# Attention with V stationary and spread reciprocals, and with the merge's operand splits placed while attention and merge run

## What is computed

```python
h = rms_norm(x, norm1_g) * (1 + sc1) + sh1
qa, ka, va, qb, kb, vb, ga, gb = jnp.split(h @ w_in, SPLIT_POINTS, axis=-1)
# global attention: 8 query heads on 2 key/value heads of 64, softmax over all keys of the group
oa = global_attention(rope(qa), rope(ka), va) @ w_branch_a
# windowed attention: a tile of queries sees its own and the two neighbour tiles, with a bias and a sink
ob = window_attention(qb * 64**-0.5, kb, vb, rel_bias, sink) @ w_branch_b
merged = jax.nn.sigmoid(ga) * oa + jax.nn.sigmoid(gb) * ob
x = x + gt1 * (merged @ w_out)
h2 = rms_norm(x, norm2_g) * (1 + sc2) + sh2
x = x + gt2 * expert_choice_moe(h2, ...)      # 16 experts, 160 rows each
y = rms_norm(x, norm_f_g)
```

## Time and profile before

| | us |
|---|---|
| median of 3 runs | 2703.78 |
| lowest and highest run | 2701.26, 2705.55 |
| the profiled execution, its own time | 2707.09 |
| its span | 2705.0 |
| TensorE busy | 2472.5 (91%) |
| DVE, ACT, POOL busy | 1634.4, 1168.9, 1016.8 |

### The profile page before, as it was taken

The page is one execution under the profiler, slowest core; times in us unless marked ns, Lnnn a source line. Parts: engine busy times, 40 slices in busy tenths (PEclk is TensorE's granted clock), DMA queues, the critical chain, the costliest instruction groups (busy, mean ns, idle before and its releaser), DMA issues.

```text
span 2705.0 us, 53532 instructions
## 1 busy us (share of the span) xinstructions
PE 2472.5 (91%) x23338; PEld 1817.1 (67%) x23428; DVE 1634.4 (60%) x2045; ACT 1168.9 (43%) x1461; POOL 1016.8 (38%) x641
## 2 busy tenths in 40 slices
PE   6999899999879999994389999999999999999994
PEld 2444578876645555553388888888888888888872
DVE  2443355544541111557588887888888888888872
ACT  2111244444531110233155556555656555566552
POOL 0000000000003232103365766676766677766640
PEclk8999699997989999996699999999999999999997
DMA  8000200012030110335288999999999999999965
GB/s 306 16 24 1 86 1 1 1 63 94 32 102 24 47 47 0 117 117 186 82 288 315 322 334 321 320 319 333 320 332 319 319 326 330 328 325 321 313 258 183
DMA packets 230112, 512.20 MB, mean 189 GB/s; under 512 B 7820, under 2 KB 35581, under 8 KB 229757
## 3 DMA queue, kind: packets, MB, share of 16 engines
q1 hardware_dynamic: 219324, 477.36, 49.8%
q0 software_dynamic: 10560, 31.46, 4.2%
HBM read 480.49 MB, written 28.31 MB: 188 GB/s over the span
## 4 chain that ended last, share of the span: by engine, by line
PE 86%; DVE 7%; ACT 2%; DMA 2%; issue 2%; SPq 1%; POOL 1%; DVEq 0%; ACTq 0%; POOLq 0%
PE ps L1337 20%; PE ps L1338 19%; PE ps L1336 19%; PE ps L1405 8%; PE ps L1472 6%; PE ps L1607 3%; PE ps L1459 3%; PE ps L1440 3%; PE ps L1450 1%; DVE arena L981 1%; DVE ti_s L990 1%; DVE top_s L989 1%; DVE arena L991 1%; PE ps L1370 1%; PE ps L1544 1%
## 5 line engine op out<-in xcount | busy, mean ns | idle before, releaser
L1337 PE MATMUL ps<-arena 128*128 128x160 bf16 (+2 forms) x5344 | 1311.2, 264 | 23.4 <-issue 8.0
L1338 PE MATMUL ps<-arena 128*128 128x160 bf16 (+2 forms) x5343 | 1310.4, 264 | 0.0
L1336 PE MATMUL ps<-arena 128*128 128x160 bf16 (+2 forms) x5255 | 1277.7, 262 | 14.9 <-DVE arena L1270 7.2
L1237 DVE TENSOR_TENSOR arena<-arena 128x2048 bf16<-128x2048 f32 x376 | 922.0, 2457 | 189.1 <-ACT arena L737 188.4
L737 ACT ACTIVATE arena<-arena 128x2048 bf16<-128x2048 f32 x384 | 726.4, 1904 | 237.1 <-PE ps L1338 180.6
L1336 PEld LDWEIGHTS ps<-arena 128*128 128x128 bf16 x5344 | 524.8, 98 | 164.4 <-issue 38.0
L1338 PEld LDWEIGHTS ps<-arena 128*128 128x128 bf16 x5344 | 524.9, 98 | 129.1 <-issue 4.2
L1337 PEld LDWEIGHTS ps<-arena 128*128 128x128 bf16 x5344 | 524.9, 98 | 120.3 <-issue 3.6
L620 POOL TENSOR_TENSOR arena<-arena 128x512 f32<-128x512 f32 (+1 forms) x24 | 26.1, 1086 | 989.9 <-DVE arena L1177 989.9
L661 POOL TENSOR_TENSOR arena<-arena 128x320 bf16<-128x320 f32 x128 | 277.8, 2170 | 10.0
L658 POOL TENSOR_TENSOR arena<-arena,ones 128x320 bf16<-128x320 f32 x128 | 182.4, 1425 | 184.2 <-DVE arena L1270 184.0
(11 more groups left out here) (192 smaller groups left out, 2211.9 us busy)
## 6 DMA issues: line engine op xcount, KB each, us to landing
arena<-w_e_gate SPq DMA_DIRECT2D x64, 2048.0 KB, 8.9
arena<-w_e_up SPq DMA_DIRECT2D x64, 2048.0 KB, 9.4
arena<-w_e_down SPq DMA_DIRECT2D x64, 2048.0 KB, 8.9
arena<-w_ada SPq DMA_DIRECT2D x12, 2048.0 KB, 8.2
arena<-x_sample SPq DMA_DIRECT2D x16, 512.0 KB, 3.5
arena<-w_in SPq DMA_DIRECT2D x16, 512.0 KB, 4.6
arena<-w_in SPq DMA_DIRECT2D x3, 2048.0 KB, 16.8
arena<-w_out SPq DMA_DIRECT2D x2, 2048.0 KB, 9.2
```

The lines of the kernel that those rows point to most:

```text
L1237: ve.tensor_tensor(lo, stage_half(kind, a), hi, ALU.subtract).then_inc(lo_done, 1)
L1336: pe.matmul(out, w_hi, x_hi, start=start, stop=False)
L1337: pe.matmul(out, w_hi, x_lo, start=False, stop=False)
L1338: return pe.matmul(out, w_lo, x_hi, start=False, stop=stop)
```

## The change

- `PV`: `V` (128x64) becomes stationary and `PT` (128 columns) moving. The two heads go to the two column halves of the array, alternating within each key tile. Bank 4 now has the head's channels on the partitions, which is the layout that `OT` made before.
- The reciprocals then have to lie along the free dimension. New step `RB`: DVE takes the reciprocal as soon as the group's exponentials are done, and POOL spreads it to 128x512 (one tensor_tensor). `OT` becomes four float32 matmuls with that tile stationary and the identity moving; ACT copies their result to `on`. `NM` on DVE multiplies bank 4 with it. `OT` now stands ahead of the last `PV` of its group.
- The bfloat16 split of the attention output goes from ACT and DVE to POOL (two tensor_tensor for each group), and so does the split of `h`: ten pairs of 128x1024, at every odd item from 51 to 69.
- `AR` stands at every second item from 34 to 48, and `AC` right behind the next item's `S` and `MX`.
- The first merge weights are loaded before attention and split behind item 80's copies, ahead of the last item's. `GT` moves behind output tile 0. `WO` 1 is done with `WO` 0, before the last chunk of the merge, and output tile 0 waits for the first 23 chunks only.
- `PT` of B and other buffers get places of their own.

```diff
@@ plan_steps
-    for i in range(len(items) + 5):
+    for i in range(len(items) + 4):
...
+        copies = [("TE",) + x[1:] for x in parts]
+        done = i - (4 if i <= first_b + 4 else 5)
+        if done >= 0 and done % NPAIR == 0 and done < len(items) and (done < first_b) == (i <= first_b + 4):
+            s.append(("RB", done // NPAIR))
...
         if i < len(items):
             s += [("S", i), ("MX", i)]
+        if s_ac < c:
+            s.append(("AC", s_ac))
+            s_ac += 1
...
-        if ready:
+        if pv < len(items) and pv <= (t - 2 if parts else t - 1):
+            if pv % NPAIR == NPAIR - 1:
+                s.append(("OT", pv // NPAIR))
             s.append(("PV", pv))
             pv += 1
...
-        if i >= first_b + 2 and i % 4 == 2 and c < 12:
+        if i >= first_b - 6 and i % 2 == 0 and c < 12:
             s.append(("AR", c))
             c += 1
-    s.append(("A2",))
...
+        if i >= first_b + 11 and i % 2 and hs < NT:
+            s.append(("HS", hs))
+            hs += 1
+        if i == len(items):
+            s += [("A2",), ("WS", 0)]
...
+                if k == "RB":
+                    g = s[1]
+                    if g:
+                        gp.wait_ge(t_done, job_at[(("OT", g - 1), 0)] + 1)
...
+                    gp.wait_ge(rinv_ready, g + 1)
+                    gp.tensor_tensor(rb_of(g).rearrange("p (h d) -> p h d", d=HD),
+                                     ones[:, 0:HD].unsqueeze(1).to_broadcast([P, 8, HD]),
+                                     rinv[:, g % 2].unsqueeze(2).to_broadcast([P, 8, HD]), ALU.mult).then_inc(rb_ready, 1)
...
+                if k == "HS":
...
+                    gp.tensor_tensor(hTs[:, 0:KD, a:z], hT[:, :, a:z], ones[:, 0:KD].unsqueeze(2).to_broadcast([P, KD, P]),
+                                     ALU.mult).then_inc(hs_hi, 1)
+                    gp.wait_ge(hs_hi, t + 1)
+                    gp.tensor_tensor(hTs[:, KD:2 * KD, a:z], hT[:, :, a:z], hTs[:, 0:KD, a:z], ALU.subtract).then_inc(hs_done, 1)
...
                 if k == "NM":
                     g = s[1]
...
+                    ve.wait_ge(rb_copied, g + 1)
                     ve.wait_ge(pv_done, NPAIR * (g + 1))
...
+                    ve.tensor_tensor(on_of(g), ps[:, 4], on_of(g), ALU.mult).then_inc(o_norm, 1)
...
-                            ins = pe.matmul(ps[:, 4, o:o + HD], PT[:, i % 2, hh, n, :], V[:, br, kt, hh * HD:hh * HD + HD],
-                                            start=(n == 0), stop=(n == len(kts) - 1))
+                    for n, kt in enumerate(kts):
+                        for hh in range(2):
+                            ins = pe.matmul(ps[hh * 64:hh * 64 + 64, 4, j * P:(j + 1) * P],
+                                            V[:, br, kt, hh * 64:hh * 64 + 64], PTs[br][:, i % 2, hh, n, :],
+                                            start=(n == 0), stop=(n == len(kts) - 1), tile_position=(0, 64 * hh))
...
-                    pe.wait_ge(o_norm, g + 1)
+                    pe.wait_ge(rb_ready, g + 1)
...
-                        ins = pe.transpose(b[:, j * P:(j + 1) * P], oh[:, g % 2, j * P:(j + 1) * P], ident[:])
+                        ins = pe.matmul(b[:, j * P:(j + 1) * P], rb_of(g)[:, j * P:(j + 1) * P], ident[:],
+                                        start=(j == 0), stop=True, skip_group_check=True)
```

## The result

The changed kernel takes **2605.7 us** (median of 4 runs, 2604.1 to 2607.1) beside 2702.5 us (2699.8 to 2705.6) for the kernel before on the same chip: a ratio of 0.9641, 95% interval 0.9625 to 0.9658. The forecast was 2620 us with a range of 2597 to 2665: sign and range held, and it was 14 us too careful.

What follows compares the result with a forecast made beforehand. TensorE's work was taken to bound A, and a chain of TensorE, ACT and DVE to bound B. From 2703.8 us, -35.4 (A) - 31.3 (B) - 17.7 (to the merge) + 0.6 = -83.8 gave 2620, range 2597 to 2665.

Steps and rivals of the forecast that it cites:

- B: Later stretch of attention, where TensorE, ACT and DVE wait for each other: forecast -31.3 us in all.
- 16 rounds and a switch: `PV` in A: column halves run side by side, 16 x 0.11 plus tile-shape switch, about 2.04 us, 1.47 less.
- A: Sample part of attention with TensorE full: forecast -35.4 us, including about -3.5 for the first items.
- The first nine items: Start of attention, called first ten items in the prediction: `PV` of 8 records at half clock, about -3.5 us.
- I take a third of the half-clock loss back, -6: Clock term in B: TensorE moves as many columns in less time, -6 us, bounds +15 and -15.
- the five `AC`: Term in B: the other five `AC` no longer stand ahead of scores, freeing about 1 us each, -5.
- It fits, barely: POOL in B: 12.4 us of work for four items against the 13.3 us they should take.
- The rival: POOL becomes B's bound: passes 2.9 times as long beside DVE, +108 us, about 2728; chance 0.05.
- To the merge: From attention's last scores to the merge's first chunk: about 14.5 us instead of 32.2, -17.7.
- From the merge to the output: `GT` behind output tile 0 costs 3.5 us; tile 0 not waiting for the last chunk saves 3; +0.6.
- the halves didn't take turns: Rival on `PV`: its column halves take turns, so it keeps 3.5 us and pays the switch, +67, 2687; chance 0.08.
- the first rival: TensorE's clock falls in B: half the last 32 items at half clock +30, 2650; all, 2686; chance 0.15.

Runs made afterwards that it cites:

- e1: The changed kernel with each item's `PV` matmuls issued all for the even head first, then all for the odd head, not alternating: 2653.1 us.
- p2: The kernel before with only the `V`-stationary `PV` and alternating column halves, its output scaled and laid out wrongly: 2639.4 us.
- p1: The kernel before with only `AR` moved to every second item from 34 to 48 and `AC` right behind the scores: 2698.6 us.
- e2: The changed kernel with `AC` issued at the end of the iteration again, behind the values: 2604.9 us.
- e6: The changed kernel with the split of `h` taken from POOL and put back on ACT and DVE behind attention, in three pieces: 2614.6 us.
- e5: The changed kernel with POOL doing each split of `h` twice: 2636.3 us.
- e9: The changed kernel with the first merge weights loaded after the last values and split at the end of attention's steps: 2615.4 us.
- e8: The changed kernel with `OT` right behind the scores and the last `RB` ahead of the first merge weights' split: 2592.3 us.
- e7: The changed kernel with `OT` issued right behind the scores and maxima, its ACT copy ahead of the exponentials: 2597.7 us.

## Why the prediction was right, and where it was off

**`PV`.** Right, and for the reason given. 16 rounds and a switch were to take 2.04. `PV` fills 1.90 and the transposes on either side take 0.14 longer than in the earlier trace rows (0.58 and 1.46 from start to start, in place of 0.49 and 1.41), so together they are the 2.04. The item is 5.86 (forecast 5.87), and e1 shows it is the alternation of halves that does it. The choice between the two rows, `AR` in column groups against the old `PV`, was the decision of this case. The rule of the Trainium skill that stood against it (TensorE: Matmul & The Clock Gate, Part 3, "The mechanism"), taken as strictly as the prediction put it, is not what these runs show: both orders of e1 and after use all rows, and alternating column halves alone brought 3.25 down to 1.90.

**A.** Right: -32.2 against -31.9. An item with `OT` takes 6.80 (forecast 6.9), `AR` and `AC` together 2.9 in A, as in the earlier trace rows.

**The first nine items.** Term mis-sized: -8.9 against -3.5. The stretch of half clock in which attention starts is 20.5 us shorter. Before, and after:

```profile
292.60:333.60 41.00, 32.14 (x128) 23.73 (x130) 15.83 (x47) 13.38 (x44) 0.00 (x0) 0.50 0.34 121
```

```profile
293.60:314.10 20.50, 12.22 (x54) 7.60 (x54) 9.72 (x33) 7.60 (x23) 0.00 (x0) 0.50 0.96 301
```

The prediction took half clock for all these items as given. p2 and e1 both have the short stretch, p1 doesn't: V stationary brings it, in either order. Beside that, `PV` itself is some 0.7 us shorter at half clock in both (1.05 and 1.06 in place of 1.74). How the -8.9 divide between the two wasn't measured, and why the clock rises sooner stays open.

**B.** Direction right, one step too small: -41.4 against -31.3. The rhythm was met (13.37 us for four items at the end of B, forecast 13.3; two items 6.19, forecast 6.1 to 6.6), `AR` and `AC` alone gave 13.0 (p1; forecast 9.3 and 5), the values alone 14.1 (p2; forecast 8 and 3). The failing step is "I take a third of the half-clock loss back, -6": all of it came back, B has no half clock left where it had 54.6 us, and what neither part brings alone is 14.3. Which piece of the change does that stays open. The reason given for the five `AC` isn't the right one: standing ahead of the scores costs nothing in the changed kernel (e2), where they stand in other items than `OT` but for one; the wait that they shed was for a bank behind `OT` (p1, p2).

**POOL.** "It fits, barely" holds (11.4 us of work, forecast 12.4, in the 12.3 us of the fastest four items), and e6 shows a cover without any leak. The rival had its place right, as e5 shows from doubled splits on; its price rested on a row of POOL beside a DVE pass with two `arena` operands, which B hardly has: in B the passes took 1.04 and 1.16 for 512 columns, as alone, and 1.90 and 2.13 for 1024.

**To the merge.** Right: 15.25 against 14.5, -16.9 against -17.7. e6 and e9 confirm the two covers. The wait that was named, the last reciprocal behind DVE's pass over the weights, was called free since the chunk "needs the weights anyway". It wasn't: DVE's pass ended at 672.4, the first chunk came at 676.8, and e8 gained 4.5 us by taking this wait away.

**From the merge to the output.** -2.1 against +0.6. TensorE's 4.58 us wait for POOL ahead of the output is gone; in its place stand two of 1.27 and 1.10 for DVE's split of `w_out`. `GT` costs 4.0 at full clock, 0.5 more than forecast. These don't add up to -2.1, and the rest wasn't looked into.

**The rivals.** The clock didn't fall in B, the halves didn't take turns (e1 shows what that would have cost: 47 us and not 67), POOL didn't bind. The worst end of the first rival was added up wrongly: 32 items at 1.9 us more give 2681, not 2686; and `OT` in A comes to +2.8 by its own numbers, not +3.0. The wait that was named last, `NM` behind ACT's copy, is there with 1.86 us, but late in B it doesn't hold up the next maximum as feared; what `OT`'s place cost was 8 us (e7), at least in part on TensorE.

## What to carry to other kernels

Matmuls whose weights lie in different column halves ran nearly side by side here when they alternated (1.90 us in place of 3.25), so two narrow outputs are worth interleaving step by step, and not one after the other. A prediction of a stretch with pauses should be made once at full and once at half clock, since removing pauses can bring back the whole difference and not a share of it. Work moved to an idle engine was free here at 93% of the loop's period and cost all that stood over beyond it, so compare its sum with the period; and where a long pass moves ahead of a short one that starts a chain over three engines, put the short one first. A wait in the trace isn't a cost by itself: look whether the instruction behind it would have waited for something else anyway, as with `NM` here.

## What the runs showed of the hardware that was not expected

- 16 float32 matmuls of 128x64 tiles moving 128 columns, 32 records, take 1.90 us with alternating column halves and 3.25 us half by half, so 0.102 for each record in a row of the same half and 0.119 for a pair across both. Eight such records take the same in either order (1.05 and 1.06 us at half clock).
- With V stationary the half clock at the start of attention lasted 20.5 us in all twelve kernels that have it, and with the probabilities stationary 41.0 and 37.5 us (before, p1).
- POOL at 93% of the loop's period in the fastest group of four items didn't slow the loop by 0.1 us. Where TensorE waited 4.1 to 5.1 us for it (e5, four times), seven us around the wait had a granted clock of 0.51 to 0.54 each time. In p2 the clock fell to half within 1.5 us behind six of seven waits of 1.31 to 1.73 us ahead of `AC`, but not behind a transpose's wait of 1.74, so the length of the wait alone doesn't decide it.
